# The triangular inverse of a chunk on 64-row corner tiles, joined by substitution

## What is computed

```python
def step(S, inp):
    r_t, w_t, a_t, b_t, v_t, k_t = inp
    sa = jnp.einsum('bhij,bhj->bhi', S, a_t)
    S = S * w_t[:, :, None, :] + sa[..., None] * b_t[:, :, None, :] + v_t[..., None] * k_t[:, :, None, :]
    return S, jnp.einsum('bhij,bhj->bhi', S, r_t)
```

## Time and profile before

| | |
|---|---|
| median of 3 runs | 1234.52 us (1233.52 to 1234.73) |
| span of the profiled execution, first to last instruction | 1230.0 us |
| PE busy | 1153.6 us (94%), 6036 matmul instructions |
| DVE busy | 412.9 us (34%) |
| ACT busy | 203.0 us (17%) |
| POOL busy | 89.3 us (7%) |
| mean granted TensorE clock | 0.991 |

### The profile page before, as it was taken

How to read it: one execution, slowest core, us unless ns; L and a number is a source line. 1 busy time by engine, 2 the same in 40 slices (tenths; PEclk the granted TensorE clock), 3 DMA queues, 4 the chain that set the end, 5 groups by cost and what they waited for, 6 DMA issues and landing times.

```text
span 1230.0 us, 15212 instructions
## 1 busy us (share of the span) xinstructions
PE 1153.6 (94%) x6036; PEld 548.2 (45%) x6036; DVE 412.9 (34%) x939; ACT 203.0 (17%) x450; POOL 89.3 (7%) x120
## 2 busy tenths in 40 slices
PE   6999999999999999998999998989999899999997
PEld 3886898774433433333333333333433333333432
DVE  0698778774412121221212121212132121212123
ACT  2311334243110101011111111010101111111102
POOL 1002664330000000000000000000000000000000
PEclk9999999999999999999999999999999999999999
DMA  9901724677999999999999999999999999999996
GB/s 372 387 24 47 311 92 172 275 240 279 358 418 427 431 430 433 434 432 426 431 434 432 426 434 431 432 423 427 430 432 436 427 427 432 436 427 425 427 426 265
DMA packets 40086, 456.43 MB, mean 371 GB/s; under 512 B 5056, under 2 KB 5584, under 8 KB 16496
## 3 DMA queue, kind: packets, MB, share of 16 engines
q1 hardware_dynamic: 39256, 455.01, 88.3%
q0 software_dynamic: 480, 0.80, 0.3%
q10 hardware_dynamic: 312, 0.11, 0.0%
HBM read 454.56 MB, written 1.34 MB: 371 GB/s over the span
## 4 chain that ended last, share of the span: by engine, by line
PE 55%; DMA 40%; DVE 3%; issue 1%; ACT 1%; SPq 0%; DVEq 0%; ACTq 0%
DMA ring<-in_w_gu 35%; PE bank L628 25%; PE bank L666 6%; PE bank L748 5%; DMA front<-in_w_down 3%; PE bank L583 2%; DMA ring<-in_ada_w 2%; PE bank L866 2%; PE bank L856 2%; PE bank L971 2%; PE bank L865 1%; PE bank L573 1%; PE bank L758 1%; PE bank L743 1%; PE bank L805 1%; PE bank L608 1%
## 5 line engine op out<-in xcount | busy, mean ns | idle before, releaser
L628 PE MATMUL bank<-ring,front 128*64 128x512 f32 x2032 | 458.0, 606 | 36.7 <-DMA ring<-in_w_gu 36.7
L628 PEld LDWEIGHTS bank<-ring,front 128*64 128x64 f32 x2032 | 143.6, 139 | 348.9 <-issue 281.3
L1459 DVE TENSOR_SCALAR front<-bank 128x512 f32<-128x512 f32 x32 | 22.1, 692 | 479.0 <-PE bank L628 479.0
L666 PE MATMUL bank<-front 128*64 128x512 f32 x512 | 113.6, 596 | 9.5 <-ACT front L1102 9.1
L666 PE MATMUL bank<-ring,front 128*64 128x512 f32 x512 | 113.4, 595 | 5.1 <-ACT front L1102 5.1
L1094 ACT ACTIVATE front<-front 128x512 f32<-128x512 f32 x32 | 20.2, 630 | 485.5 <-DVE front L1459 485.5
L1483 DVE COPY front<-bank 64x512 f32<-64x512 f32 x32 | 21.9, 683 | 175.1 <-PE bank L666 175.1
L666 PEld LDWEIGHTS bank<-front 128*64 128x64 f32 x512 | 36.3, 137 | 76.5 <-issue 73.3
L666 PEld LDWEIGHTS bank<-ring,front 128*64 128x64 f32 x512 | 36.3, 137 | 71.9 <-issue 70.4
L583 PE MATMUL bank<-front 128*128 128x512 f32 x136 | 62.9, 605 | 1.3 <-DVE front L1483 1.3
L1577 DVE SCALAR_TENSOR_TENSOR front<-front 128x286 f32<-128x286 f32 x120 | 58.8, 540 | 0.5
(11 more groups left out here) (263 smaller groups left out, 1001.1 us busy)
## 6 DMA issues: line engine op xcount, KB each, us to landing
ring<-in_w_gu SPq DMA_DIRECT2D x46, 4096.0 KB
front<-in_w_down SPq DMA_DIRECT2D x30, 2048.0 KB, 19.7
ring<-in_w_down SPq DMA_DIRECT2D x28, 2048.0 KB, 20.1
ring<-in_w_gu SPq DMA_DIRECT2D x25, 2048.0 KB
ring<-in_ada_w SPq DMA_DIRECT2D x24, 1024.0 KB, 10.6
ring<-in_w_gu SPq DMA_DIRECT2D x20, 1024.0 KB
ring<-in_w_in SPq DMA_DIRECT2D x5, 2048.0 KB, 20.0
ring<-in_w_down SPq DMA_DIRECT2D x6, 1024.0 KB, 9.5
```

The costliest lines, as they stand in the source:

```text
L628: last = pe.matmul(ps[r][64 * hf:64 * hf + 64, :], xT[:, k, S * q:S * q + S], rows, start=False, stop=(k == order[-1]))
L666: last = pe.matmul(ps[2][64 * c:64 * c + 64, :], actT[:, m, 64 * hf:64 * hf + 64], wdn[q][hf][:, m, c * 512:(c + 1) * 512], start=(k == 0) ...
```

## The change

The inverse is formed only for the two diagonal 64-row blocks of each system. `LEVELS` goes from 7 to 6. The tiles of the inverse (`YX`, `IL`, `LTn`, `Pn`, the masks) keep 128 partitions but have 64 columns: rows 0 to 63 hold the first block, rows 64 to 127 the second. Each matmul of a level becomes two, one for each block, on its own 64x64 corner of the array. `join_ways` adds the two triangles into the compact tile `LC` in two instructions of 64 rows. `LTn` has one buffer for each level. What joined the blocks in the last level is now done by substitution, in three rounds with a copy after each: `near_sums` (the block that each direction meets first, and the identity times W of the other), `cross_sums` (the product across the blocks), `far_sums` (the other block's inverse). `near_sums` is copied by ACT and DVE (`take_near`), cross by ACT into `Tm`, far by ACT in two instructions for each g. `ada_part` is moved behind `far_sums`, the V-by-`LT` outputs between near and cross. `norm_var` of chunks 1 and 2 stands between cross and far. `TAPS_BEFORE` goes from 3 to 4, and the bonus and convolution sums move to other levels.

```diff
-LEVELS = 7
+LEVELS = 6
+HB = 64
-TAPS_U, TAPS_K, TAPS_R, TAPS_BEFORE, TAPS_BESIDE = (12, 16, 16), 8, 5, 3, (1, 1, 1)
+TAPS_U, TAPS_K, TAPS_R, TAPS_BEFORE, TAPS_BESIDE = (12, 16, 16), 8, 5, 4, (1, 1, 1)
...
-            sp.wait_ge(s["sa_mm"], 2 * Q)
+            sp.wait_ge(s["sa_mm"], 6 * Q)
             load_dn_rows(1, 0, 3)
...
             def level_product(q, lv, c):
...
-                pe.matmul(ps[c % 2][:, 0:T], LTn[:, lv % 2, g, h, :], YX[:, c, 1, :], start=True, stop=True)                    .then_inc(s["p_mm"], 1)
+                for rows in halves:
+                    last = pe.matmul(ps[c % 2][rows, 0:HB], LTn[rows, lv - 1, g, h, :], YX[rows, c, 1, :],
+                                     start=True, stop=True)
+                last.then_inc(s["p_mm"], 1)
...
             def level_update(q, lv, c):
...
                 if lv < LEVELS - 1:
-                    pe.matmul(ps[2 + c][:, T:2 * T], YX[:, c, 0, :], Pn[:, c, :], start=False, stop=False, skip_group_check=True)
-                pe.matmul(ps[2 + c][:, 0:T], Pn[:, c, :], YX[:, c, 0, :], start=False, stop=(lv == LEVELS - 1),
-                          skip_group_check=True).then_inc(s["e_mm"], 1)
+                    for rows in halves:
+                        pe.matmul(ps[2 + c][rows, HB:2 * HB], YX[rows, c, 0, :], Pn[rows, c, :],
+                                  start=False, stop=False, skip_group_check=True)
+                for rows in halves:
+                    last = pe.matmul(ps[2 + c][rows, 0:HB], Pn[rows, c, :], YX[rows, c, 0, :],
+                                     start=False, stop=(lv == LEVELS - 1), skip_group_check=True)
+                last.then_inc(s["e_mm"], 1)
+
+            def near_sums(q, g):
+
+                pe.wait_ge(s["w_ev"], 2 * q + g + 1)
+                if g == 0 and q > 0:
+                    pe.wait_ge(s["bo"], q)
+                if g == 0 and q == Q - 1:
+                    pe.wait_ge(s["gn_std"], q)
+                if g == 1 and q == Q - 1:
+                    pe.wait_ge(s["c_std"], 3)
+                for rows, d in zip(halves, (1, 0)):
+                    pe.matmul(ps[6 + g][rows, 0:P], ident[rows, rows], W[rows, g, d, :],
+                              start=True, stop=False, skip_group_check=True)
+                pe.wait_ge(s["yx_ev"], 26 * q + 20 + 2 * g + 2)
+                for h in range(2):
+                    for rows, d in zip(halves, (0, 1)):
+                        last = pe.matmul(ps[6 + g][rows, 2 * P + h * HD:2 * P + h * HD + HD], XM[rows, 2 * g + h, 0, :],
+                                         W[rows, g, d, h * HD:h * HD + HD], start=False, stop=True, skip_group_check=True)
+                last.then_inc(s["sa_mm"], 1)
+
+            def cross_sums(q, g):
+
+                pe.wait_ge(s["sa_ev"], 6 * q + g + 1)
+                pe.wait_ge(s["yx_ev"], 26 * q + 24 + g + 1)
+                for h in range(2):
+                    for to, of, d in ((1, 0, 0), (0, 1, 1)):
+                        last = pe.matmul(ps[6 + g][halves[to], h * HD:h * HD + HD], LT[halves[of], g, h, d, 3, halves[to]],
+                                         SA[halves[of], g, d, h * HD:h * HD + HD], start=False, stop=True, skip_group_check=True)
+                last.then_inc(s["sa_mm"], 1)
+
+            def far_sums(q, g):
+
+                pe.wait_ge(s["sa_ev"], 6 * q + 2 + g + 1)
+                for h in range(2):
+                    for rows in halves:
+                        last = pe.matmul(ps[6 + g][rows, 3 * P + h * HD:3 * P + h * HD + HD], XM[rows, 2 * g + h, 1, :],
+                                         Tm[rows, g, h * HD:h * HD + HD], start=False, stop=True, skip_group_check=True)
+                last.then_inc(s["sa_mm"], 1)
...
+                for g in range(G):
+                    cross_sums(q, g)
+                if 0 < q < Q - 1:
+                    norm_var(q - 1, ps[4])
+                for g in range(G):
+                    far_sums(q, g)
+                if q < 2:
+                    ada_part(q, True, True)
+                elif q == 2:
+                    ada_part(2, True, False)
+                    ada_part(3, False, True)
...
                 for g in range(G):
-                    a.wait_ge(s["sa_mm"], 2 * q + g + 1)
-                    a.activation(SA[:, g].rearrange("p d i -> p (d i)"), ps[6 + g][:, 256:512], ACT.Copy)\
+                    a.wait_ge(s["sa_mm"], 6 * q + g + 1)
+                    a.activation(SA[halves[0], g, 0, :], ps[6 + g][halves[0], 2 * P:3 * P], ACT.Copy).then_inc(s["sa_ev"], 1)
+                for g in range(G):
+                    a.wait_ge(s["sa_mm"], 6 * q + 2 + g + 1)
+                    a.activation(Tm[:, g, :], ps[6 + g][:, 0:P], ACT.Copy).then_inc(s["sa_ev"], 1)
+                for g in range(G):
+                    a.wait_ge(s["sa_mm"], 6 * q + 4 + g + 1)
+                    a.activation(SA[halves[0], g, 1, :], ps[6 + g][halves[0], 3 * P:4 * P], ACT.Copy)
+                    a.activation(SA[halves[1], g, 0, :], ps[6 + g][halves[1], 3 * P:4 * P], ACT.Copy)\
                         .then_inc(s["sa_ev"], 1)
                 if 0 < q < Q - 1:
                     norm_std(q - 1, ps[4])
```

More of the change, by code:

```diff
@@ L196, in build @@
         LT = view(ring[:, 16384:20480], "p (g h d k t) -> p g h d k t", g=G, h=2, d=2, k=4)
[L200 to L207, removed]
+        YX = view(ring[:, 20480:20992], "p (c a t) -> p c a t", c=2 * G, a=2)
+        XM = view(ring[:, 20992:21504], "p (c w t) -> p c w t", c=2 * G, w=2)
+        IL = view(ring[:, 21504:21760], "p (g h t) -> p g h t", g=G, h=2)
+        LC = view(ring[:, 21760:22016], "p (g h t) -> p g h t", g=G, h=2)
+        LTn = view(ring[:, 22016:23296], "p (n g h t) -> p n g h t", n=LEVELS - 1, g=G, h=2)
+        Pn = view(ring[:, 23296:23552], "p (c t) -> p c t", c=2 * G)
+        Tm = view(r_L[:, 1536:1792], "p (g n) -> p g n", g=G)
+        halves = [slice(HB * b, HB * b + HB) for b in range(2)]
+        mask_homes = (r_mask, r_mid[:, 0:384])
+        masks = [home[:, n * HB:(n + 1) * HB] for home in mask_homes for n in range(home.shape[1] // HB)]
         side_mask, level_mask = masks[0:LEVELS - 1], masks[LEVELS - 1:2 * (LEVELS - 1)]
+        end_mask = view(mask_homes[1][:, 4 * HB:6 * HB], "p (w t) -> p w t", w=2)
         W, SA = (view(ring[:, 23552 + 512 * n:24064 + 512 * n], "p (g d i) -> p g d i", g=G, d=2)
@@ L923, in _ @@
                 for g in range(G):
[L924 to L937, removed]
-                if 0 < q < Q - 1:
-                    norm_var(q - 1, ps[4])
-                if q < 2:
-                    ada_part(q, True, True)
-                elif q == 2:
-                    ada_part(2, True, False)
-                    ada_part(3, False, True)
+                    near_sums(q, g)
                 for g in range(G):
@@ L1361, in _ @@
             po.wait_ge(s["kv_mm"], len(items) - 19)
-            po.tensor_copy(IL.rearrange("p g h t -> p (g h) t"), ident.unsqueeze(1).broadcast_to([P, 4, P])).then_inc(s["il_id"], 1)
+            for rows in halves:
+                po.tensor_copy(IL[rows].rearrange("p g h t -> p (g h) t"),
+                               ident[rows, rows].unsqueeze(1).broadcast_to([HB, 2 * G, HB])).then_inc(s["il_id"], 1)
             def sum_bonus(q):
@@ L1706, in _ @@
                         conv_taps(TAPS_BESIDE[q])
[L1707 removed]
+                    if lv == 2 and q > 0:
                         norm_bonus(q - 1)
[L1709 removed]
+                    if lv == LEVELS - 1:
+                        for g in range(G):
+                            take_near(q, g)
+                    if q == Q - 1 and lv in (2, 3):
                         v.wait_ge(s["cs_mm"], 2)
[L1712 removed]
+                        for c in (2 * lv - 4, 2 * lv - 3):
                             v.scalar_tensor_tensor(acc[:, c, :], ps[7][:, 0:A_COLS], -1.0 / CH, acc[:, c, :],
@@ L1892, in constants, with own @@
     lower = i[:, None] >= i[None, :]
-    side = [np.where((i[:, None] >> n) % 2 == 0, lower, lower.T) for n in range(1, LEVELS)]
+    side = [np.where((i[:, None] >> n) % 2 == 0, lower, lower.T) for n in range(1, LEVELS + 1)]
     blocks = [(i[:, None] >> n) ^ (i[None, :] >> n) == 1 for n in range(LEVELS)]
-    lv = blocks[0].astype(np.float32)
-    part = np.stack(side + blocks[1:], axis=1).astype(np.float32)
+    def own(m):
+        return np.concatenate([m[0:HB, 0:HB], m[HB:P, HB:P]])
+    lv = own(blocks[0]).astype(np.float32)
+    ends = [side[-1].T, side[-1]]
+    part = np.stack([own(m) for m in side[:-1] + blocks[1:] + ends], axis=1).astype(np.float32)
     return c, lv, part
```

111 lines of the change are left out of this document (57 added, 54 removed).

## The result

The changed kernel takes 1216.51 us (median of 4 runs, 1215.93 to 1217.23), the kernel before 1234.16 on the same chip: a ratio of 0.9852, 95% interval 0.9839 to 0.9866. The forecast was 1218.5, and the mechanism is the likeliest case (d).

What follows compares the result with a forecast made beforehand. The experts' stage was taken as bound by weight transfers, the recurrence ahead of it by TensorE. Chunk savings of 5.2, 2.7, 4.8 and 3.3 make 16.0 us: span 1230.0 to 1214.0, plus 4.5 around it, 1218.5 us; range 1208 to 1233.

Steps and rivals of the forecast that it cites:

- case (d): Whole kernel: the forecast's own mechanism holds, 1218.5 us, own range 1212 to 1225; chance 0.62.
- What bounds the kernel: Experts' stage bound by weight transfers; time taken out of the recurrence ahead of it comes off the end almost whole.
- sign of transfers that bound earlier: Would show the forecast wrong: the shift at the recurrence's end is larger than at the span's end.
- Passes: Levels of the inverse: 48 64x64 passes at 0.03 us, 1.4 us a level, replace 24 at 0.112.
- rival (a): Levels: corner tiles take turns, 0.055 us per pass, a level 2.64 us, about 0 saved, 1234; chance 0.17.
- Rival (b): Levels: 64x64 passes cost more than 0.06 us and the change loses; at 0.08, 1260 us; chance 0.06.
- Inverse: Five level periods of 2.70 us become four of 1.9; saves 6.7, 6.4, 6.4 and 5.4 us in chunks 0 to 3.
- VectorE nearly full: Beside each level, four evictions at 0.285 us, a tap of 0.51 and gaps fill about 1.8 us.
- the first and the last part: Inverse before and after the periods: first keeps its length despite three shape changes; last goes from 2.16 to 1.35 us.
- Tail: Sums in three rounds, with shape changes and copy waits: 1.5 us lost in chunk 0, 1.6 in 1 and 2, 2.1 in 3.
- The stall in chunk 1: Square root behind the sums' copies delays VectorE; first eviction at 14.9 us against TensorE's 12.6, 2.1 us of stall.
- GpSimd and the late SP load: Masks come before they are needed; chunk 3's convolution squares cost 0 to 1 us; the later load has room.

Runs made afterwards that it cites:

- one-corner run: Changed kernel with the updates' passes for rows 64 to 127 replaced by second passes on the corner of rows 0 to 63: 1221.82 us, one run.
- transfers held: Changed kernel with the second half (4 MB) of the first modulation weights issued only when chunk 0's far sums are done: 1215.04 us.
- long filler: Changed kernel with five matmuls of 512 columns, results unused, before the third products of chunk 2, in TensorE's wait: 1216.36 us.
- early-norm run: Changed kernel with `norm_var` and the square root `norm_std` of chunks 1 and 2 moved directly behind the near sums: 1211.8 us.
- short filler: Changed kernel with three matmuls of 512 columns, results unused, before the third products of chunk 2, in TensorE's wait: 1213.52 us.

## Why the prediction was right, and where its terms were off

**What bounds the kernel.** Right. The recurrence's 16.7 us came off the span to 15.9; with a level left out it was 7.0 of 8.7. The 0.8 that the experts' stage gave back was not in the sum (the shift at the recurrence's end larger than at the span's end was named as a sign of transfers that bound earlier). Where in that stage it is lost I did not isolate.

**Passes, and rival (a).** 0.029 us against 0.03. The rival's mechanism, tiles that take turns, is what the one-corner run made: 0.0575 per pass (its price had been 0.055), a period of 2.3. The real corners overlap although both write one bank. What the one-corner run leaves open is whether its passes wait for the corner or for the columns that both matmuls write there. The page TensorEngine Tiling (Array Packing) of the Trainium skill, Gotcha 1, says that different row tiles cannot access the same PSUM bank simultaneously. The trace disagrees for this layout, in which the two tiles write different partition halves of the bank; two row tiles that write the same partitions were not tried. Rival (b) falls with this; its threshold was a little low by its own rows (136 full passes at 0.112 against 224 corner passes are 0.068 us a pass, not 0.06), which changes nothing.

**Inverse: 27.5 saved where 24.9 were forecast.** The period of 1.76 instead of 1.9 gives 4 x 0.14 = 0.6 per chunk. The rival cause of the period, VectorE nearly full, is out (taps moved, period unchanged). The prediction counts the first and the last part from the weight load of the second product, 0.05 to 0.11 us ahead of its matmul; counted so, the first part took 2.31 us where 2.83 were kept, 0.5 more saved: the changes of shape there cost less than the smaller passes gave. The last part is 1.91 instead of 1.35, 0.6 less saved. Together chunk 0 saves 7.2 where 6.7 stood. In chunk 3 the five insertions cost less than thought (6.3 against 5.4).

**Tail: the price of three rounds was a little high, and one thing was missing.** Without the wait for issue and the low clock chunk 0's tail is 10.6 us (transfers held): 1.2 over the 9.37 of before, forecast 1.5. Chunks 1 to 3 lost 1.1, 1.2 and 1.7 where 1.6, 1.6 and 2.1 stood. The missing term is the step from 10.6 to 13.6 us in chunk 0: instructions that come late under full transfers, and half the clock behind it. The run with the long filler, which changes nothing ahead of chunk 2's products, has the wait without the low clock:

```profile
140.19 0.44 PE L897 MATMUL bank<-ring,front 64*64 64x128 f32 x4 [1.00 <-issue]
```

Its clock is 1.00 from 139 to 145 us and its tail 11.8. So the wait costs 1.2 us there, and of the step of 3.0 about 1.5 goes to the wait of 1.27 and about 1.5 to the low clock. In the early-norm run, with a wait of 0.91 and the clock at 1.00, the tail is 11.1, but there another 1.0 us was lost before it, in the inverse (12.3 instead of 11.3), with a wait for issue of 0.21 and one of 0.69 for VectorE; so it doesn't show that the wait is cheap.

**The stall in chunk 1: right in its mechanism, under-sized.** 2.1 were forecast, 3.8 measured. The late root itself, from sums to sums, is worth 33.6-30.9 = 2.7 (transfers held, clock full, against early norm); TensorE was ready for VectorE at 12.2 us (the products' start at 182.41, 11.0 behind the sums, and 1.2 to an eviction as in chunk 0), not at 12.6, and the few tenths of room were not there. The low clock costs another 1.4, gone with the short filler. That makes 4.1; from the products of the kernel before it is 3.8, since the corner tiles had made this stage shorter too (7.7 instead of 8.15 in chunks 0 and 2, 0.5 each, which the sum had left out).

**GpSimd and the late SP load.** The masks and the load cost nothing that shows: no wait of TensorE in the levels names the masks. But a later GpSimd instruction does show. The last tap among the levels takes 1.4 us in chunks 0 to 2 (the mean of all taps is 0.54), and each time it lies over this one and ends 0.3 us behind it:

```profile
136.89 1.26 POOL L1395 TENSOR_TENSOR front<-front 128x512 f32<-128x512 f32 x1
...
137.07 1.40 DVE L1631 SCALAR_TENSOR_TENSOR front<-front 128x286 f32<-128x286 f32 x1
```

The last evictions stand behind that tap, and TensorE waits 0.37 to 0.38 us for them in each of these chunks' sums. In the early-norm and the short-filler run the long tap came one level earlier in chunk 0, and TensorE waited 0.7 for it. No run moved this instruction.

So the span came out within 0.1 us of the sum because errors cancel: 2.6 more from the inverse and 0.3 at the start, against 1.4 more lost in the tails, 0.8 more in the products and 0.8 given back by the experts. That part is luck.

## What to carry to other kernels

- Half-size corner tiles pay when the loop they stand in is bound by passes: a pass fell from 0.112 to 0.029 us, the level only from 2.70 to 1.76, since then the round trip to the copying engine sets it. Look for that loop before splitting further.
- When a stage gets more rounds of copies, look at what is queued behind them on the copying engine. Here one square root, with the stall and the low clock behind it, was worth about 4 us; the rounds themselves cost 1.1 to 1.7 per chunk.
- Price a stall of TensorE above its length: what runs behind it may run at half the clock. And size a filler by the wait: three matmuls took 1.4 us off that stretch, five nothing.

## What the hardware showed that was not expected

- TensorE waited 0.91 to 2.96 us for instructions ("issue") at the end of chunk 0, in a stretch where transfers kept the DMA engines full and the program had many small matmuls; with half the transfers held it did not.
- After TensorE had stood still for 1.3 to 5 us its granted clock was 0.50 (1.2 GHz) for about 3 us in several executions, and in others, after waits of 0.91 to 1.00, 2.51 and 2.94 us, it stayed at 1.00.
- Two 64x64 tiles on opposite corners that write the two partition halves of one bank overlap fully: 0.029 us per pass against 0.0575 on one corner.
- A VectorE tap that takes 0.51 us by itself took 1.39 to 1.61 when it lay over a GpSimd instruction of 128x512 elements, and ended 0.3 us behind it.
